# Memory attention: GpSimd in place of ScalarE scales the probabilities, and both layers are written out in the program

## The reference

```python
for l in range(DEPTH):                       # DEPTH = 2
    x = x + mixers(rmsnorm(x)) @ w_out[l]    # latent attention, 8 heads, and a spatial gating MLP
    h = rmsnorm(x, norm_mem_g[l])
    m = rmsnorm(mem, mem_norm_g[l])          # 256 memory tokens
    x = x + memory_attention(h, m, w_mq[l], w_mkv[l], w_mo[l])
    x = x + conv_ffn(rmsnorm(x, norm_ffn_g[l]))

def memory_attention(h, mem_h, w_mq, w_mkv, w_mo):      # 4 heads of 256
    s = einsum('bqhd,bmhd->bhqm', q, k) * (MEM_HEAD_DIM ** -0.5)
    p = softmax(s, axis=-1)
    o = einsum('bhqm,bmhd->bqhd', p, v)
    return o @ w_mo
```

## Time and profile before

| | |
|---|---|
| median of 3 runs (lowest, highest) | 1600.33 us (1597.85, 1602.95) |
| the profiled execution | 1602.88 us |
| its span, first to last instruction | 1601.1 us |
| mean granted TensorE clock | 0.97 |
| busy: PE, DVE, ACT, POOL | 1488.0, 773.9, 760.9, 696.0 us |
| share of the span | 93%, 48%, 48%, 43% |

### The profile page before, as it was taken

How to read it: one execution, slowest core, us unless ns; L and a number is a source line. 1 busy time by engine, 2 the same in 40 slices (tenths; PEclk the granted TensorE clock), 3 DMA queues, 4 the chain that set the end, 5 groups by cost and what they waited for, 6 DMA issues and landing times.

```text
span 1601.1 us, 20864 instructions
## 1 busy us (share of the span) xinstructions
PE 1488.0 (93%) x6846; PEld 1215.6 (76%) x6846; DVE 773.9 (48%) x1264; ACT 760.9 (48%) x1187; POOL 696.0 (43%) x327
## 2 busy tenths in 40 slices
PE   4988879998999999999999787999989999999995
PEld 3766658877878888888877565798778888888883
DVE  4547767815165431255162866783423654114543
ACT  5676645536254432344356765463634443224431
POOL 3374415840434454434536362376123534544350
PEclk9998899999999999999999888999999999999997
DMA  4320013530213332222322101244111323322221
GB/s 167 116 66 27 14 53 119 184 105 1 97 61 106 105 111 100 80 89 94 123 92 94 41 14 40 82 155 148 50 53 66 103 94 105 117 94 85 86 79 53
DMA packets 39048, 138.91 MB, mean 87 GB/s; under 512 B 4848, under 2 KB 5104, under 8 KB 38704
## 3 DMA queue, kind: packets, MB, share of 16 engines
q1 hardware_dynamic: 37440, 134.23, 24.7%
q10 hardware_dynamic: 1520, 3.52, 0.7%
HBM read 135.64 MB, written 2.10 MB: 86 GB/s over the span
## 4 chain that ended last, share of the span: by engine, by line
PE 50%; issue 30%; POOL 17%; DVE 1%; ACT 1%; POOLq 0%; DVEq 0%; ACTq 0%
PE ps L1316 16%; PE ps L1317 16%; PE ps L1318 16%; POOL w_lo L342 12%; POOL arena L362 1%; POOL work L355 1%; POOL work L356 1%; POOL work L357 1%; POOL h_lo L367 0%; PE ps L1466 0%; DVE work L1299 0%; DVE work L885 0%; ACT arena L556 0%; ACT work L533 0%; PE ps L1326 0%
## 5 line engine op out<-in xcount | busy, mean ns | idle before, releaser
L342 POOL TENSOR_TENSOR w_lo<-raw,w_hi 128x1024 fp32r<-128x1024 f32 x248 | 603.1, 2449 | 768.5 <-ACT w_hi L444 767.0
L1316 PE MATMUL ps<-h_hi,w_hi 128*128 128x512 f32 (+2 forms) x1040 | 409.4, 394 | 25.4 <-POOL w_lo L342 22.4
L444 ACT ACTIVATE w_hi<-raw 128x1024 fp32r<-128x1024 f32 x248 | 255.6, 1055 | 323.5 <-PE ps L1318 322.4
L1318 PE MATMUL ps<-h_hi,w_lo 128*128 128x512 f32 (+2 forms) x1040 | 405.1, 390 | 0.0
L1317 PE MATMUL ps<-h_lo,w_hi 128*128 128x512 f32 (+2 forms) x1040 | 405.0, 389 | 0.0
L1316 PEld LDWEIGHTS ps<-h_hi,w_hi 128*128 128x128 f32 (+1 forms) x1040 | 196.1, 189 | 69.4 <-issue 22.6
L1316 PE MATMUL ps<-arena,w_hi 128*128 128x512 f32 (+2 forms) x656 | 247.7, 378 | 0.0
L1317 PE MATMUL ps<-arena,w_hi 128*128 128x512 f32 (+2 forms) x656 | 245.3, 374 | 0.0
L1318 PE MATMUL ps<-arena,w_lo 128*128 128x512 f32 (+2 forms) x656 | 244.5, 373 | 0.0
L1317 PEld LDWEIGHTS ps<-h_lo,w_hi 128*128 128x128 f32 (+1 forms) x1040 | 196.1, 189 | 41.0 <-issue 1.0
L1318 PEld LDWEIGHTS ps<-h_hi,w_lo 128*128 128x128 f32 (+1 forms) x1040 | 196.0, 188 | 40.8
(11 more groups left out here) (175 smaller groups left out, 1913.4 us busy)
## 6 DMA issues: line engine op xcount, KB each, us to landing
raw<-blocks_d SPq DMA_DIRECT2D x248, 512.0 KB, 3.3
x<-xT_d SPq DMA_DIRECT2D x4, 512.0 KB, 8.7
work<-memT_d ACTq DMA_DIRECT2D x2, 1024.0 KB, 4.9
outT_d<-work SPq DMA_DIRECT2D x8, 256.0 KB, 2.2
work<-ln_d ACTq DMA_DIRECT2D x2, 512.0 KB, 3.4
par<-par_d ACTq DMA_DIRECT2D x2, 113.5 KB, 2.0
work<-pos_d ACTq DMA_DIRECT2D x1, 128.0 KB, 7.0
mix_g<-par_d ACTq DMA_DIRECT2D x2, 4.0 KB, 6.6
```

Source lines behind the costliest of these rows:

```text
L342: gp.tensor_tensor(w_lo[:, b % SPLIT, :], raw[:, b % RAW, :], w_hi[:, b % SPLIT, :].bitcast(F32), ALU.subtract).then_inc(lo_done.sem, 1)
L444: act.activation(w_hi[:, b % SPLIT, :], raw[:, r, :], ACT.Copy).then_inc(hi_done.sem, 1)
L1316: pe.matmul(out, a_hi, b_hi, start=first, stop=False)
L1318: return pe.matmul(out, a_lo, b_hi, start=False, stop=last)
```

## The change

GpSimd's stream gets 16 scalings `mprobs` per layer, between the low parts of the blocks up to B_MO + 2 and those from B_MO + 3 on; ScalarE's stream loses them, and its steps i of the memory attention are otherwise in the same order. [...] And on GpSimd, ScalarE, VectorE and TensorE the loop over the layers is a Python loop: the program holds both layers, and `l` is a number. The inner loops stay.

```diff
@@ GpSimd, layer(l)
-                lows(B_OUT + 3, BLOCKS - (B_OUT + 3))
-
-            with gp.Fori(0, DEPTH) as l:
+                lows(B_OUT + 3, B_MO + AHEAD - (B_OUT + 3))
+
+                def mprobs(i):
+                    need(mrecip_done, i + 1)
+                    gp.tensor_tensor(em[:, i % 4, :], em[:, i % 4, :],
+                                     rin[:, i % 4:i % 4 + 1].to_broadcast([P, N_MEM]), ALU.mult)\
+                        .then_inc(mprob_done.sem, 1)
+
+                for i in range(MEM_HEADS * TT):
+                    mprobs(i)
+                lows(B_MO + AHEAD, BLOCKS - (B_MO + AHEAD))
+
+            for l in range(DEPTH):
                 layer(l)
@@ ScalarE, layer(l)
-                def mprobs(i):
-                    need(mrecip_done, i + 1)
-                    act.activation(em[:, i % 4, :], em[:, i % 4, :], ACT.Copy, scale=rin[:, i % 4:i % 4 + 1])\
-                        .then_inc(mprob_done.sem, 1)
...
                 for i in range(3):
                     mexps(i)
-                mprobs(0)
                 for i in range(MEM_HEADS * TT):
                     h, t = divmod(i, TT)
-                    if i + 1 < MEM_HEADS * TT:
-                        mprobs(i + 1)
                     if i + 3 < MEM_HEADS * TT:
                         mexps(i + 3)
                     mturned_hi(i)
...
-            with act.Fori(0, DEPTH) as l:
+            for l in range(DEPTH):
                 layer(l)
@@ VectorE and TensorE
-            with dve.Fori(0, DEPTH) as l:
+            for l in range(DEPTH):
...
-            with pe.Fori(0, DEPTH) as l:
+            for l in range(DEPTH):
```

## The result

Median of six runs: **1591.39 us** (1588.36 to 1592.98). The kernel before, six runs beside them: 1601.2 us (1597.85 to 1603.57). The ratio is 0.9938, 95% interval 0.9921 to 0.9956: faster by 0.6%.

What follows compares the result with a forecast made beforehand. TensorE was taken as saturated in the MLP stretch, with waits in the attentions, few on the moved scaling. Terms -0.6 - 1.28 - 1.5 = -3.4 us took the median of 1600.33 to 1596.9 us; range 1592 to 1602.

Steps and rivals of the forecast that it cites:

- The table load: Start of layer 1: ScalarE loses the table load ahead of its first weight split, so the first matmul comes 1.28 us earlier.
- Register arithmetic: Latent attention: without address arithmetic before waits, engines start sooner after stalls; 0.75 us per layer, -1.5 us in all.
- The rival in which all 238 steps count: All 238 arithmetic steps of 32 ns on L1309 lie on the path: -7.6 us, ending at 1590.8 us; chance 0.13.
- The scaling: Memory attention: 16 scalings per layer go from ScalarE to GpSimd at 0.71 us each; 0.3 us per layer, -0.6 us.
- step 12's gain: Memory attention: transposes 12 get their scaling 0.45 us sooner, given back at once as transposes 13 wait for VectorE's L1191.
- The relieved steps 1 to 5: Memory attention: relieved of scaling, ScalarE no longer bounds; VectorE's 0.98 us per step is the new pace, 0.4 us gained.
- The jump back: End of layer 1's loop pass: TensorE's branch of 3.39 us lies in a saturated stretch, so removing it gains 0.
- the hold: Memory attention: GpSimd's scalings stop VectorE through their shared port; costed at 0, as a rival 1620.2 us, chance 0.03.
- a rival, as a loss that longer stalls might bring: GpSimd sets the memory attention's pace (0.10) and, in a third of that, the clock falls by 0.1: 1609.5 us.
- -3.6 us (all waits on L718 gone): Memory attention: best bound of the scaling term, if every TensorE wait ending at ScalarE's scaling L718 vanished.
- My own condition for being wrong: Forecast wrong if memory attention changes by over 2 us, L1013 or L1012 grow, or idle time without a releaser appears.

Runs made afterwards that it cites:

- the filled runs: Extra unread matmuls in TensorE's longest waits of latent and memory attention, on the kernel before, the changed kernel and each part alone; filled kernel before 18.5 us faster.
- run 9: Kernel before with extra unread matmuls in the waits of both attentions, plus the layers in full on ScalarE alone: 1579.65 us.
- run 13: Changed kernel with the 1.28 us table load put back ahead of the first weight split: 1592.68 us against 1591.68.
- run 1: Kernel before with only the layers in full on all four engines, scaling still on ScalarE: 1597.53 us, ratio 0.9987.
- runs 3 and 4: Extra unread matmuls in TensorE's waits of the memory attention only: on the kernel before 1595.14 us (ratio 0.9968), on the changed kernel 1589.45 us (0.9933).
- runs 5 and 8: Extra unread matmuls in the waits of both attentions: on the kernel before (1580.8 us), and with only the scaling moved to GpSimd (1.9 us less).
- run 5: Kernel before with extra unread matmuls in TensorE's longest waits of latent and memory attention, some overrunning their wait: 1580.8 us, ratio 0.9880.
- run 15: Kernel before with extra unread matmuls in the waits of both attentions, cut so they no longer overrun: 1575.54 us.
- run 2: Kernel before with only the scaling moved to GpSimd, layer loops kept: 1598.26 us, ratio 0.9981.
- run 11: Changed kernel with extra unread matmuls in the waits of both attentions, GpSimd doing each scaling twice: 1581.28 us, +4.5.

## Why the prediction was wrong

The sum of its terms was about right and a term was missing. With the waits filled the change is worth 3.0 to 4.1 us, for the 3.4 that the terms gave. That match is in part luck: in the filled runs the layers in full gave 2.2 us for a forecast 2.8, the scaling 1.9 for 0.6, and the two misses cancel.

- *The table load, -1.28.* Right: 1.3 us at the first matmul in run 9, 1.0 us of the time in run 13. In the profiled pair 1.8, since the first table load on ScalarE was also 0.5 us earlier; the two profiles of the changed kernel differ by as much (first matmul at 19.83 and 20.25).
- *Register arithmetic, -1.5.* The mechanism is right, the size somewhat too large: the waits of latent attention lose 1.0 us in layer 1, and with fills the three other engines give 1.0 us in all. TensorE's start behind L1006 and L362, in the changed kernel:

```profile
132.38 0.67 DVE L1008 TENSOR_TENSOR arena<-ps,arena 64x512 fp32r<-64x512 f32 x1
...
133.11 0.80 PE L1318 MATMUL ps<-arena 96*128 96x512 f32 x1 [4.24 <-DVE arena L1008]
```

```profile
146.89 1.26 POOL L362 TENSOR_TENSOR arena<-work,arena 32x512 fp32r<-32x512 f32 x1
...
148.25 0.47 PE L1318 MATMUL ps<-arena 96*128 96x512 f32 x1 [2.57 <-POOL arena L362]
```

  That is 0.06 us and 0.10 us after the release, for 0.13 and 0.23; I expected 0.05 and 0.14. The rival in which all 238 steps count, 7.6 us, fell to run 1. That its time, 1590.8, is the one that came out is chance.
- *The scaling, -0.6.* Right in mechanism (L397 at 0.615 us for my 0.71; GpSimd's queue free; step 12's gain lost to VectorE's pair), too small in size: 0.5 us per layer within the stage by runs 3 and 4, where I took 0.3 (and my own steps add up to 0.4). The filled runs 5 and 8 give 1.9 us in all; what brings the other 0.9, outside the memory attention, was not found. The relieved steps 1 to 5 now follow at TensorE's 0.93 us rather than VectorE's 0.98.
- *The jump back, 0, and the hold, 0.* Right: 433 us as before, L1015 unchanged.
- *The failed step* is what I did with the clock. I read 0.91 in the stage and used it only in a rival, as a loss that longer stalls might bring. I wrote "-3.6 us (all waits on L718 gone)" as the bound of a faster stage and so put at nothing that a matmul behind a wait can cost twice. The groups at 1.2 GHz stood in the trace, 0.43 us apart. In the profiled pair layer 1's memory attention gave 3.8 us where I had 0.3, and about 3.2 of it are two products that rose to 2.4 GHz; of the whole gain of 8 to 10 us, all beyond the 3.0 to 4.1 goes when the waits are filled. My own condition for being wrong, a memory attention that changes by over 2 us, named the place.
- *What stays open.* Why low clock leaves the memory attention of layer 1 and not of layer 2, and why the scaling alone is under 1597 us in five of 12 executions while both parts together are under 1596 in all 12; that its other seven have low clock in that stage is likely but not shown. What is left of -8 beside -1.5 and -0.7 is the clock's, since with fills the parts add up; which of the waits decides was not isolated.

The Trainium skill, "TensorE: Matmul & The Clock Gate", section "Part 1: The HAM clock gate", says that a gate sets TensorE's clock by how busy it has been of late. The filled kernels agree: with more work in the waits the mean clock rises from 0.972 to 0.994. Here the low clock of the memory attention stood behind waits of 0.91 and 0.93 us, and in the changed kernel, with equal waits in both layers, it stood in one layer and not in the other.

## What to carry to other kernels

Before pricing a change in a stage with waits, list the matmuls there that start at twice their usual distance, and price them as a term of its own with both signs: a shorter wait may give back the matmuls behind it as well. To find what a change is worth by itself, compare both kernels with the waits filled by matmuls that nobody reads; here that turned 6 us that no part had alone into a plain sum. The filling is a speed-up in itself: 1.2% on the kernel before where it overruns some waits (run 5, ratio 0.9880, 0.9862 to 0.9898), 1.6% where it is cut to end inside them (run 15, ratio 0.9843, 0.9830 to 0.9857).

## What was not expected of the hardware

- Low clock costs far more than the change was about: filling the waits made the kernel before 18.5 us faster, 24 with the fills cut to fit (1599.8 to 1575.5).
- Two executions of one program can be 8 us apart and what the runs show of them is only the granted clock (run 2: 1591.1 at 0.976, 1599.7 at 0.972).
- GpSimd's 128x256 product with a repeated operand takes 613 to 617 ns in all 32 cases, a quarter of its 128x1024, with no fixed part to be seen. Back to back in run 11 they start 0.57 us apart.
